# MLP products and retention queries and keys as two streams over the array's lower and upper 64 rows

## What is computed

```python
def _mlp(x, norm_g, w1, w2):                      # x 256x1024, w1 1024x4096, w2 4096x1024
    h = _rmsnorm(x, norm_g)
    return jnp.square(jax.nn.relu(h @ w1)) @ w2

def _odd_mixer(x, norm_g, w_in, ...):             # w_in 1024x6144
    h = _rmsnorm(x, norm_g)
    q, k, v, g = _split(h @ w_in, ODD_SPLITS)     # q and k: 1024 columns each
    ...

for layer in range(2):
    x = x + mixer(layer, x)
    x = x + _mlp(x, mlp_norm[layer], w_mlp_in[layer], w_mlp_out[layer])
```

## Time and profile before

| | before |
|---|---|
| median of three runs | 973.98 us (973.87 to 974.19) |
| the profiled execution: time, span | 973.81 us, 972.0 us |
| granted TensorE clock, mean | 0.999 |
| busy: PE, PEld (weight loads), DVE, ACT, POOL | 99%, 85%, 72%, 57%, 16% |
| products on PE | 5352 |

### The profile page before, as it was taken

One profiled execution on the slowest core, in us unless ns is written; L12 is line 12 of the kernel. 1 busy time (PEld: TensorE's weight loads), 2 busy tenths in 40 slices (PEclk: granted clock), 3 DMA queues, 4 the chain that ended last, 5 costly groups with the idle time before them and its releaser, 6 DMA issues.

```text
span 972.0 us, 14012 instructions
## 1 busy us (share of the span) xinstructions
PE 963.9 (99%) x5352; PEld 829.2 (85%) x5352; DVE 702.5 (72%) x1085; ACT 552.2 (57%) x949; POOL 154.9 (16%) x189
## 2 busy tenths in 40 slices
PE   9999999999999999999999999999999999999997
PEld 8878888888888888888888888888888889988885
DVE  6788676776666767786667656666758989778884
ACT  6688665444555553455456444554535857766662
POOL 2741018920001102220001000000550110000000
PEclk9999999999999999999999999999999999999999
DMA  9985535565554663345455665555544453543631
GB/s 342 301 218 190 182 132 179 187 231 183 173 194 156 216 214 131 130 135 211 174 174 181 203 212 185 173 190 182 208 153 147 157 190 114 191 131 130 216 130 44
DMA packets 110338, 174.73 MB, mean 180 GB/s; under 512 B 4288, under 2 KB 73024, under 8 KB 110272
## 3 DMA queue, kind: packets, MB, share of 16 engines
q1 hardware_dynamic: 109840, 173.40, 53.5%
q10 hardware_dynamic: 432, 0.44, 0.1%
HBM read 172.78 MB, written 1.05 MB: 179 GB/s over the span
## 4 chain that ended last, share of the span: by engine, by line
PE 96%; DVE 3%; issue 1%; ACT 0%; POOLq 0%; POOL 0%; DVEq 0%; ACTq 0%
PE ps L572 24%; PE ps L542 14%; PE ps L445 10%; PE ps L447 9%; PE ps L446 9%; PE ps L546 7%; PE ps L500 7%; PE ps L509 4%; PE ps L521 2%; PE ps L700 1%; PE ps L680 1%; PE ps L530 1%; PE ps L668 1%; PE ps L624 1%; DVE arena L1668 1%
## 5 line engine op out<-in xcount | busy, mean ns | idle before, releaser
L1556 DVE TENSOR_TENSOR wlo<-raw,whi 128x1024 fp32r<-128x1024 f32 x312 | 373.9, 1237 | 16.5 <-PE ps L572 8.3
L1047 ACT ACTIVATE whi<-raw 128x1024 fp32r<-128x1024 f32 x312 | 315.6, 1048 | 34.8 <-PE ps L572 22.0
L572 PE MATMUL ps<-whi,ur 128*128 128x512 f32 x656 | 182.0, 390 | 0.0
L572 PEld LDWEIGHTS ps<-whi,ur 128*128 128x128 f32 x656 | 121.1, 188 | 23.5
L542 PE MATMUL ps<-hT,whi 128*128 128x512 f32 x592 | 140.5, 389 | 0.0
L542 PEld LDWEIGHTS ps<-hT,whi 128*128 128x128 f32 x592 | 110.8, 188 | 22.8
L445 PE MATMUL ps<-whi,hT 128*128 128x512 f32 (+1 forms) x312 | 122.0, 391 | 0.0
L447 PE MATMUL ps<-whi,hT 128*128 128x512 f32 (+1 forms) x312 | 120.0, 385 | 0.0
L446 PE MATMUL ps<-wlo,hT 128*128 128x512 f32 (+1 forms) x312 | 119.9, 384 | 0.0
L1923 DVE TENSOR_TENSOR arena<-ps,arena 128x256 f32<-128x256 f32 x80 | 33.4, 423 | 98.6 <-ACT arena L1289 98.6
L1289 ACT ACTIVATE arena<-ps 128x256 f32<-128x256 f32 x80 | 30.2, 385 | 127.2 <-PE ps L546 127.2
(11 more groups left out here) (233 smaller groups left out, 1384.4 us busy)
## 6 DMA issues: line engine op xcount, KB each, us to landing
raw<-in_w SPq DMA_DIRECT2D x64, 1024.0 KB, 5.6
raw<-in_w_in SPq DMA_DIRECT2D x34, 1024.0 KB, 4.9
raw<-in_w_in_o SPq DMA_DIRECT2D x24, 1024.0 KB, 5.2
raw<-in_w_out_o SPq DMA_DIRECT2D x8, 1024.0 KB, 4.8
raw<-in_w_in_e SPq DMA_DIRECT2D x5, 1024.0 KB, 13.0
raw<-in_w_mem SPq DMA_DIRECT2D x4, 1024.0 KB, 9.4
raw<-in_w_out_e SPq DMA_DIRECT2D x4, 1024.0 KB, 4.8
raw<-in_w_out SPq DMA_DIRECT2D x4, 1024.0 KB, 4.8
```

The costliest lines, as they stand in the source:

```text
L572: mm = e.matmul(bank("acc", stage, 2 * tb + i), x[p], t[p % 2][:, 0, 512 * i:512 * i + 512], start=start and p == 0, stop=stop and p == 2)
L1047: e.activation(split_half(i)[0], raw_half(i), ACT.Copy).then_inc(*up("hi", ("hi", i)))
L1556: e.tensor_tensor(l, raw_half(i), h.bitcast(F32), ALU.subtract).then_inc(*up("lo", ("lo", i)))
```

## The change

`t_pair` splits every k-tile of 128 rows into rows 0 to 63 (`LOWER`) and 64 to 127 (`UPPER`). For each k-tile and half of the tile there are three pairs of products of 256 columns: high weight x high activation, low x high, high x low. The lower product of a pair sums into one bank, the upper one into another, both halves of the tile side by side in a bank. ACT copies the lower bank as a whole (`lower_copied`), and DVE adds the upper one (`upper_added`).

`acc_rows` takes the place of `acc_half` in the MLPs, except for the last tile. Lower and upper rows sum into the same four banks, but never into one bank at once: in turn 0 the lower rows write columns 0 to 511 and the upper rows columns 512 to 1023, in turn 1 the other way round. Before each group of six products PE waits until both streams' group before on the same two banks has ended. The two streams count semaphores of their own, and the weight buffers wait for both.

```diff
@@ t_pair
-                hl, o = [split_half(first_half[label] + m) for m in range(2)], [take("mm", label, m) for m in range(2)]
+                lower, upper = take("mm", label, 0), take("mm", label, 1)
                 for m in range(2):
-                    w.wait_ge(*at("hi", first_half[label] + m))
+                    i, c = first_half[label] + m, slice(256 * m, 256 * m + 256)
+                    h, l = weights(i)
                     for k in range(8):
                         w.wait_ge(*at(*x_split(stage, k)))
-                        e.matmul(o[m], hl[m][0][:, k, :], hTs[:, k * 512:k * 512 + 512], start=k == 0, stop=False)
-                for m in range(2):
-                    w.wait_ge(*at("lo", first_half[label] + m))
-                    for k in range(8):
-                        mm = e.matmul(o[m][:, 0:256], hl[m][1][:, k, :], hT[0][:, k, :], start=False, stop=k == 7)
-                    mm.then_inc(*up("mm", ("mm", label, m), ("wd", first_half[label] + m)))
-                    give("mm", label, m)
+                        for p, (t, x) in enumerate(((h, hT[0]), (l, hT[0]), (h, hT[1]))):
+                            start, stop = k == 0 and p == 0, k == 7 and p == 2
+                            a = e.matmul(lower[:, c], t[LOWER, k, :], x[LOWER, k, :], start=start, stop=stop)
+                            b = e.matmul(upper[:, c], t[UPPER, k, :], x[UPPER, k, :], start=start, stop=stop)
+                    a.then_inc(*up("lower", ("lower", label, m), ("wd", i)))
+                    b.then_inc(*up("upper", ("upper", label, m), ("wd upper", i)))
+                give("mm", label, 0), give("mm", label, 1)
@@ new
+            def acc_rows(stage, label, x, u, d, before):
+                i = first_half[label] + x
+                t = weights(i)
+                for turn in range(2):
+                    for tb in range(2):
+                        other = (i, 0) if turn else (before, 1)
+                        if turn or before is not None:
+                            w.wait_ge(*at("lower", stage, tb, *other))
+                            w.wait_ge(*at("upper", stage, tb, *other))
+                        n = slice(tb * 128, tb * 128 + 128)
+                        for p, (y, v) in enumerate(((u[0], t[0]), (u[0], t[1]), (u[1], t[0]))):
+                            a = e.matmul(bank("acc", stage, 2 * tb + turn), y[LOWER, d + x, n], v[LOWER, 0, 512 * turn:512 * turn + 512],
+                                         start=before is None and turn == 0 and p == 0, stop=False)
+                            b = e.matmul(bank("acc", stage, 2 * tb + 1 - turn), y[UPPER, d + x, n], v[UPPER, 0, 512 - 512 * turn:1024 - 512 * turn],
+                                         start=before is None and turn == 0 and p == 0, stop=False)
+                        a.then_inc(*up("lower", ("lower", stage, tb, i, turn), ("wd", i)))
+                        b.then_inc(*up("upper", ("upper", stage, tb, i, turn), ("wd upper", i)))
+                return i
@@ mlp on PE
-                            acc_half(f"mlp{layer}", ("w2", layer, p), 0, u, d, start=p == 0)
-                            acc_half(f"mlp{layer}", ("w2", layer, p), 1, u, d)
+                            done = acc_rows(f"mlp{layer}", ("w2", layer, p), 0, u, d, done if p else None)
+                            done = acc_rows(f"mlp{layer}", ("w2", layer, p), 1, u, d, done)
@@ mlp and rq on ACT, DVE likewise with upper_added
-                        for m in range(2):
-                            low_copied(("w1", layer, j), m, rl[:, m * 256:m * 256 + 256])
+                        if j:
+                            lower_copied(("w1", layer, j), rl)
+                        else:
+                            for m in range(2):
+                                low_copied(("w1", layer, j), m, rl[:, m * 256:m * 256 + 256])
```

More of the change, by code:

```diff
@@ L35 @@
 SEMS = ["mm", "wd", "tp", "qk", "pv", "hi", "xh", "aev", "ex", "asq", "lo", "xl", "dev", "dst", "sc", "po",
-        "w0", "w1", "w2", "w3", "w4", "w5", "w6", "w7", "raw0", "raw1", "raw2", "raw3", "x0", "x1", "t0", "t1", "t2", "t3", "t4", "id", "c", "c2", "g", "b", "m", "out"]
+        "w0", "w1", "w2", "w3", "w4", "w5", "w6", "w7", "raw0", "raw1", "raw2", "raw3", "x0", "x1", "t0", "t1", "t2", "t3", "t4", "id", "c", "c2", "g", "b", "m", "out",
+        "lower", "upper"]
 PAIRS = [(0, 2), (1, 3), (4, 6), (5, 7)]
@@ L53 @@
 SP = 257
+LOWER, UPPER = slice(0, 64), slice(64, 128)
 WIDE_UP = ((0, 1), (1, 0), (1, 1), (2, 0))
@@ L178, in program @@
         NH = 2 * len(tiles)
+        by_rows = set()
+        for m, t in enumerate(tiles):
+            kind, last = t[0][0], t[0][-1]
+            if (kind in ("w1", "rq") and last > 0) or (kind == "w2" and last < 15):
+                by_rows.update((2 * m, 2 * m + 1))
         value, count, bank_of, columns = {}, {}, {}, {}
@@ L1046, in weights_to @@
                         w.wait_ge(*at("wd", i - NHI))
+                        if i - NHI in by_rows:
+                            w.wait_ge(*at("wd upper", i - NHI))
                     e.activation(split_half(i)[0], raw_half(i), ACT.Copy).then_inc(*up("hi", ("hi", i)))
@@ L1289, in low_copied, with lower_copied @@
                 e.activation(dst, bank("mm", label, m)[:, 256:512], ACT.Copy).then_inc(*up("aev", ("lc", label, m)))
+            def lower_copied(label, dst):
+                w.wait_ge(*at("lower", label, 1))
+                src = bank("mm", label, 0)
+                e.activation(dst, two(src) if label[0] == "rq" else src, ACT.Copy).then_inc(
+                    *up("aev", ("lc", label), ("free", ("mm", label, 0))))
             def mlp(layer, gcol, before):
@@ L1305, in mlp @@
                             w.wait_ge(*at("wd", first_half["w2", layer, 2 * (j // 2) - 3] + 1))
+                            w.wait_ge(*at("wd upper", first_half["w2", layer, 2 * (j // 2) - 3] + 1))
                         e.activation(u[0][:, d:d + 2, :], two(sq), ACT.Copy).then_inc(*up("xh", ("uh", layer, j)))
@@ L1335, in act_program @@
                 used(("rq", c), 1)
-                for m in range(2):
-                    low_copied(("rq", c), m, (oqT if c < 4 else okT)[:, 2 * (c % 4) + m, :])
+                if c:
+                    lower_copied(("rq", c), (oqT if c < 4 else okT)[:, 2 * (c % 4):2 * (c % 4) + 2, :])
+                else:
+                    for m in range(2):
+                        low_copied(("rq", 0), m, oqT[:, m, :])
                 if c:
@@ L1555, in weights_to @@
                         w.wait_ge(*at("wd", i - NLO))
+                        if i - NLO in by_rows:
+                            w.wait_ge(*at("wd upper", i - NLO))
                     e.tensor_tensor(l, raw_half(i), h.bitcast(F32), ALU.subtract).then_inc(*up("lo", ("lo", i)))
@@ L1924, in low_added, with upper_added @@
                     *up("dev", ("t", label, m), ("free", ("mm", label, m))))
+            def upper_added(label, d):
+                w.wait_ge(*at("lc", label))
+                w.wait_ge(*at("upper", label, 1))
+                src = bank("mm", label, 1)
+                e.tensor_tensor(d, two(src) if label[0] == "rq" else src, d, ALU.add).then_inc(
+                    *up("dev", ("t", label, 0), ("t", label, 1), ("free", ("mm", label, 1))))
             def mlp(layer):
@@ L1931, in mlp @@
                         rl, sq, u, d = RL[j % 2], SQ2[j % 2], ur[(j // 2) % 2], 2 * (j % 2)
-                        for m in range(2):
-                            low_added(("w1", layer, j), m, rl[:, m * 256:m * 256 + 256])
+                        if j:
+                            upper_added(("w1", layer, j), rl)
+                        else:
+                            for m in range(2):
+                                low_added(("w1", layer, j), m, rl[:, m * 256:m * 256 + 256])
                         if j >= 2:
@@ L1964, in dve_program @@
                 used(("rq", c), 1)
-                for m in range(2):
-                    low_added(("rq", c), m, (oqT if c < 4 else okT)[:, 2 * (c % 4) + m, :])
+                if c:
+                    upper_added(("rq", c), (oqT if c < 4 else okT)[:, 2 * (c % 4):2 * (c % 4) + 2, :])
+                else:
+                    for m in range(2):
+                        low_added(("rq", 0), m, oqT[:, m, :])
                 if c:
```

## The result

The changed kernel takes 982.62 us (median of 4 runs, 982.57 to 983.24) against 973.95 us for the kernel before on the same chip: 8.67 us more, a ratio of 1.009 with a 95% interval from 1.0073 to 1.0108. It is slower, and by what was forecast (983).

What follows compares the result with a forecast made beforehand. The prediction took the distances between matmul starts on TensorE (busy 99%) as the bound. 973.81 + 8.1 + 1.0 = 982.9 gave a forecast of 983 us, 0.9% slower, own range 979 to 988, wider range 953 to 1020.

Steps and rivals of the forecast that it cites:

- What bounds the kernel: Whole kernel: TensorE is busy 99% of the span, so time is the sum of distances between matmul starts.
- Term 1: t_pair: three 256-column products per k-tile instead of two products, 120 ns a slot, +0.22 us in each of 37 calls: +8.1 us.
- Term 2: Output products: 24 half-height ones in two streams take 12 x 228 ns a call, as before: 0.
- Term 3: New waits at bank swaps in acc_rows: hidden behind the group between, about 400 ns left for semaphores: 0.
- Term 4: Changing between full and half height: three excursions, two MLPs and one for queries and keys: +1.0 us.
- Term 5: ScalarE and VectorE: one 512-column copy and addition per call instead of two of 256 each; later, but covered: 0.
- fast rivals: Products in half-height streams: 13 ns loss vanishes (955 us, chance 0.24), or loads hide fully (971 us, 0.12).
- slow rivals: Two streams: they hinder each other at loads or issue (1015 us, chance 0.18), or don't overlap (some 1330 us, 0.10).

Runs made afterwards that it cites:

- bench: Kernel without the computation, issuing only trains of 48 products of one kind: one-pass fp32 over 128 rows settles at 226.7 ns (512 columns), 120.0 ns (256).
- e5: Changed kernel with acc_rows' two loops exchanged, so two of four groups wait for the group just before: 1035.77 us against 973.65 for the kernel before.
- e2: Kernel before with acc_rows alone, keeping the old t_pair with its copies and additions: 987.20 us against 973.54.
- e3: Kernel before with the split t_pair alone, keeping the old acc_half: 993.28 us, ratio 1.0203.

## Why the prediction was right

- **What bounds the kernel.** That PE's distances are the time held throughout: every experiment moved the total by the sum of its distances.
- **Term 1 (+8.1 us) was right in size: 7.8 us.** The slot is 120 ns. Its reason was wrong in part. The prediction began with a loss of 13 ns per product whatever its width, which is what bench shows, but term 1 then explained the 120 ns by weight loads of about 118 ns that hold the train. In bench trains of 128 columns, with the same load before each product, run at 112 ns, so a load doesn't take 118 ns of a train; and the share per column that I put in its place for bench was wrong as well. The number survived, by luck in this step, because the changed kernel uses exactly the two widths whose distances the trace of before gave. For other widths either reading would have failed.
- **Term 2 (0) was right**: 5.46 against 5.47 us, and 48 products at half height count like 24 at full height.
- **Term 3 (0) was right.** Its reserve was stated without the semaphores' own time; with it some 0.24 us are left (e5: a bare wait costs 0.44 us beyond the products, where I expected 0.35).
- **Term 4 (+1.0 us) was right**, a little small: 3 x 0.4 = 1.2 us, and e2 and e3 price it at 0.45 and 0.38 us. Had the change split only one of the two product kinds, this small term would have been the largest, 12 to 14 us.
- **Term 5 (0) was right**: ACT's wait before the copy grew from 3.5 to 4.6 us, as foretold, and reached nobody.
- **The fast rivals** fell by the same fact: a half-height product pays what a full-height one pays, alone (L75, L78 of bench) or beside its neighbour. The rule by which 256 columns take 109 ns is true for bf16 here. The rows that spoke for it, the two-stream attention scores, were two-pass products, and those lose only 2.5 ns at full height too (L89 of bench): the small loss went with the two passes, not with the streams. **The slow rivals** fell too: two streams hold each other up neither at their loads nor at their operands, and the issue is not near its limit (31 ns per product in bench).

The terms as measured, 7.8 + 1.2 = 9.0 us, stand against 8.67 us in the medians and 8.8 us in the spans (980.8 - 972.0); 0.1 us of the difference is PE's earlier arrival at the first t_pair (135.62 against 135.7), and the rest is too small to place.

## What to carry to other kernels

Splitting the depth of a full 128-row product into two streams of 64 rows gave nothing here, in one-pass fp32 and in bf16: the halves run side by side, at the distance that the whole had, and entering and leaving half height costs 0.4 us. What counts is how many products a column total is cut into, since each one-pass fp32 product of 256 to 512 columns costs 13 ns beyond its columns (with 128 columns of weights); so keep high and low activations side by side in one 512-column product, sort products by width, and if streams are needed for other reasons (small heads), keep them together in one stretch. Where streams must swap banks, put a group of products between the two turns: 0.68 us of them hid the wait here, and by the 0.44 us that it costs bare, some 0.5 us would do (an estimate; no run tried anything between none and 0.68 us).

## What I had not expected of the hardware

- The loss per one-pass fp32 product is 13.3 ns at 256, 320, 384 and 512 columns, against 2.5 ns for bf16.
- Alternating 512- and 256-column products cost 353 ns a pair instead of 347, at both heights, but not everywhere: the full array's retention pairs stayed at 347.
- Each half of a change can be dearer alone: +13.7 and +19.7 us against +8.7 us together.
- Four streams of 32 rows run at the distance of one full product, a product every 31 ns.
